# One channel tile of the convolution on GpSimd, and narrower chunk pair products, in the two mixers

## The chip, the cores and the metric

The kernel runs on one core of a Trainium2 chip. The metric is the device time of one execution in microseconds (us), of the slowest core, which here is the only one; of several runs the median counts. The engines of the core are TensorE (PE in the profile, its weight loads PEld), VectorE (DVE), ScalarE (ACT), GpSimd (POOL) and SyncE (SP, which here only issues transfers).

## What is computed

Two transformer layers with four parallel mixers each (the first followed by a dense feed-forward network, the second by a mixture of experts), and then one more block of another kind. The change is in the mixers alone, which run twice:

```python
for l in range(DEPTH):                       # DEPTH = 2, x: 256 tokens x 1024 channels
    h = _rmsnorm(x, norm_mix[l])
    p_rw, p_sb, p_ret, p_conv = jnp.split(h @ w_in[l], MIX_SPLITS, axis=-1)
    branches = (_rwkv7_mixer(p_rw, ...), _stick_breaking_mixer(p_sb, ...),
                _retention_mixer(p_ret, ...), _conformer_conv_mixer(p_conv, ...))
    merged = sum over i of jax.nn.sigmoid(h @ w_gate[l, i]) * (branches[i] @ w_branch[l, i])
    x = x + merged @ w_out[l]
    ...

def _conformer_conv_mixer(p, dw, db, ln_w, ln_b):
    u_a, u_b = jnp.split(p, 2, axis=-1)
    u = u_a * jax.nn.sigmoid(u_b)
    u = lax.conv_general_dilated(u, dw[:, None, :], ..., padding=[(CONV_WIDTH - 1, 0)],
                                 feature_group_count=BRANCH_WIDTH) + db
    return jax.nn.silu(_layernorm(u, ln_w, ln_b, CONV_LN_EPS))

def _rwkv7_mixer(p, ...):                     # 4 heads of 64 channels
    def step(state, inp):                     # one step per token
        r_t, w_t, k_t, v_t, kk_t, a_t = inp
        sa = jnp.einsum('bhvk,bhk->bhv', state, -kk_t)
        state = (state * w_t[:, :, None, :] + sa[..., None] * (kk_t * a_t)[:, :, None, :]
                 + v_t[..., None] * k_t[:, :, None, :])
        return state, jnp.einsum('bhvk,bhk->bhv', state, r_t)
```

The convolution is depthwise: every one of 256 channels has 31 weights of its own (CONV_WIDTH) and sums 31 shifted copies of its row of 256 tokens. The recurrence of the first mixer is computed by the kernel in 8 chunks of 32 tokens, from products of all pairs of tokens of a chunk.

## The kernel before

Activations lie with channels on the partitions, so the 256 channels of a branch are two tiles (index `j`) of 128 partitions by 256 tokens. Weights come from HBM as blocks of 128x1024 in a ring. A block is used in split form: ScalarE copies its rounded part (`HiParts.upto`, L343), VectorE subtracts that from the block (`LoParts.upto`, L363), and TensorE makes three products of each (`three_passes`, L270 to L272). `upto(n)` on either engine means: split all blocks up to number n that are not yet split. Each engine has its own program, written out by hand in the order in which it runs; waits are on counters of named steps (`after(name)`), and on VectorE every instruction of the mixers waits for the one before it (`link`).

The stage at issue stands in `mix_section`. TensorE runs, for each chunk c of 8, `gram(c)` and `gate(c)`. `gate(c)` projects one block of gate weights: 24 products of 128x256. `gram(c)` makes the pair products of the chunk. Its operands `KR` and `BK` hold the four heads on a block diagonal: for tile j (heads 2j and 2j+1) a 128x128 matrix whose only filled columns are the 64 of these two heads (32 tokens for each head); the rest is zero. There are four products of 128x256 into bank Z0 or Z1 (L632, 2 of w by 2 of j, the two j added up in PSUM), two of 128x128 into bank X (L639, again added over j), and four transposes (L646).

VectorE runs beside it, for each chunk c: the masked product of the bank (`gram_c`, L1067, from bank Z and constants), for c = 3 and 7 another one from bank X (`A_0`, `A_1`), the split of the block for the next gate, and four of the 31 taps of the convolution by `taps`, each for both tiles: `acc[j] = u[j] shifted by k, times weight, plus acc[j]`, one instruction on 128x256 (L1071; the first tap L1069). The input of the convolution, `u`, is finished by the instruction just ahead of this stage. The result `acc` is read first by the two instructions of `conv_y` (L1069 too), much later: behind the four steps of the inverse of chunks 0 to 3 (`inverse(0, k)`, `squares(0, k)`, `ret_s`).

After the chunks TensorE runs `ret_scores(0)` (L687, L688), then `squares(0, 1)` (L666 into bank C, L671 into bank X), `gate(8)`, and `inverse(0, 1)` (L680). L671 needs bank X, which VectorE has read when `A_1` is done. A scratch tile `at_`, which lies over `u`, is used for the weights of two of the four retention heads.

GpSimd does little: it writes zeros over `praw`, `KR`, `BK` and the margin of `u` at the start of a mixer section (L474 to L478), and scales eight tiles for the router (L1448).

Of the kernel before, what the change touches and what calls it, by code (L numbers as in the profile page):

```python
# [15 lines left out]
ALU = mybir.AluOpType  # L16
# [4 lines left out]
T = 256  # L21
# [6 lines left out]
HD = 64  # L28
# [6 lines left out]
TAPS = 31  # L35
PAD = TAPS - 1
# [94 lines left out]


SPARE_AT = 28704
PARAMS2_AT = 29120


class Plan:
# [9 lines left out]
    def done(self, engine, name=None, by=1):  # L147
        self.count[engine] += by
        if name:
            assert (self.section, name) not in self.steps, name  # L150
            self.steps[self.section, name] = (engine, self.count[engine])
        return self.sem[engine], by

    def after(self, name, section=None):
        engine, n = self.known[section or self.section, name] if self.known is not None else ("pe", 1)
        return self.sem[engine], n
# [250 lines left out]
def mix_section(env, layer):  # L407

    nc, dram, x, banks, h_hi, h_lo = (env[n] for n in ("nc", "dram", "x", "banks", "h_hi", "h_lo"))
    after, done, C, eps, ident, col, plan = (env[n] for n in ("after", "done", "C", "eps", "ident", "col", "plan"))  # L410
    first = MIX1_AT if layer else 0
    P0, P1, Z0, Z1, BO, BC, BY, BX = (banks[n] for n in ("P0", "P1", "Z0", "Z1", "O", "C", "Y", "X"))
    pair = lambda b: b.rearrange("p (j t) -> p j t", j=2)
    quad = lambda b: b.rearrange("p (j t) -> p j t", j=4)

    cut = carver(env)
    prm = env["params"][:, layer]
    R = lambda name, i=0, n=1: col(prm, PCOL, name, i, n)
# [3 lines left out]
    KR = cut(2, NCH, 2, P)  # L422
    BK = cut(2, 2, NCH, P)
# [19 lines left out]
    sbv, rv = values[:, 0], values[:, 1]  # L443
    rg, acc, scr = (cut(2, T) for _ in range(3))
    u = cut(2, PAD + T)
    az = cut(384)
    dec = cut(2, NCH)
    w0h, small = cut(4), cut(64)
    assert cut.at[0] <= SPARE_AT, cut.at[0]

    uflat, rflat = u.rearrange("p j t -> p (j t)"), rv.rearrange("p a t -> p (a t)")
    A1 = sbo.rearrange("p j t -> p (j t)").rearrange("p (i n) -> p i n", i=4)
    exz = vv.rearrange("p j t -> p (j t)")[:, 0:384]
    at_ = uflat[:, 0:384]
# [16 lines left out]
    def gpsimd(g):  # L471
        if layer:
            g.wait_ge(*after("h2_lo_3", "mix0"))
        g.memset(praw[:, :, 0:1], 0.0).then_inc(*done("pool", "praw_zeroed"))  # L474
        if layer == 0:
            g.memset(KR, 0.0).then_inc(*done("pool"))
        g.memset(BK, 0.0).then_inc(*done("pool"))
        g.memset(u[:, :, 0:PAD], 0.0).then_inc(*done("pool", "zeroed"))  # L478

    def tensor(pe):  # L480
        blocks = Blocks(env, pe, first)
# [31 lines left out]
        for k in range(KD):  # L513
# [4 lines left out]
            mm = pe.matmul(BX[:, 0:T], C("ones"), sqx[:, k, :], start=(k == 0), stop=(k == KD - 1))  # L518
# [28 lines left out]
        for j in range(2):  # L547
            mm = pe.matmul(Z0[:, j * T:(j + 1) * T], lora[0:64, j * P:(j + 1) * P], pm[0:64, 4, :], start=True, stop=True)
        mm.then_inc(*done("pe", "lora_w"))
        take(Z1, "tha")  # L550
        for j in range(2):
            mm = pe.matmul(Z1[:, j * T:(j + 1) * T], lora[64:128, j * P:(j + 1) * P], pm[64:128, 4, :], start=True,
                           stop=True)
# [9 lines left out]
        for j in range(2):  # L563
            mm = pe.matmul(BO[:, j * T:(j + 1) * T], lora[:, 256 + j * P:256 + (j + 1) * P], pm[:, 5, :], start=True, stop=True)
# [11 lines left out]
        for a in range(TT2):  # L576
            for j in range(2):
                mm = pe.transpose(BY[:, (2 * a + j) * P:(2 * a + j + 1) * P], vv[:, j, a * P:(a + 1) * P], ident)
# [48 lines left out]
        def gram(c):  # L627
            z = Z0 if c % 2 == 0 else Z1
            take(z, f"gram_{c}")
            for w in range(2):  # L630
                for j in range(2):
                    mm = pe.matmul(z[:, w * T:(w + 1) * T], BK[:, w, j, c, :],  # L632
                                   KR[:, j, c].rearrange("p w n -> p (w n)"), start=(j == 0), stop=(j == 1))
            mm.then_inc(*done("pe", f"p_gram_{c}"))

            if c % 4 == 0:
                take(BX, f"A_{c // 4}")
            for j in range(2):
                mm = pe.matmul(quad(BX)[:, c % 4, :], KR[:, j, c, 0, :], BK[:, 0, j, c, :], start=(j == 0), stop=(j == 1))  # L639
            if c % 4 == 3:  # L640
                mm.then_inc(*done("pe", f"p_A_{c // 4}"))
            o = BO if c % 2 == 0 else BC
            take(o, f"BK_{c}")
            for w in range(2):
                for j in range(2):
                    mm = pe.transpose(quad(o)[:, 2 * w + j, :], BK[:, w, j, c, :], ident)  # L646
            mm.then_inc(*done("pe", f"p_BK_{c}"))
# [43 lines left out]
        def attend(hh, values, weights, ready, out_name):  # L691

            b, j = (hh % 2) * HD, hh // 2
            pe.wait_ge(*after(ready))
            pe.matmul(BO[b:b + HD, j * T:(j + 1) * T], values[:, 0, hh * HD:(hh + 1) * HD], weights[:, 0:T],
                      start=True, stop=False, skip_group_check=True)
            pe.matmul(BO[b:b + HD, j * T + P:(j + 1) * T], values[:, 1, hh * HD:(hh + 1) * HD], weights[:, T:T + P],
                      start=False, stop=True, skip_group_check=True).then_inc(*done("pe", out_name))
# [7 lines left out]
        for k in range(1, 5):  # L706
            inverse(0, k)
            if k < 4:
                squares(0, k + 1)
            attend(k - 1, rv, az if k % 2 else at_, f"ret_s_{k - 1}", f"p_ret_o_{k - 1}")  # L710
            if k < 4:
                ret_scores(k)
            gate(8 + k)
# [17 lines left out]
        for j in range(2):  # L731
            mm = pe.matmul(Z0[:, 0:T], C("ones"), acc[:, j, :], start=(j == 0), stop=(j == 1))
# [5 lines left out]
        for j in range(2):  # L738
            mm = pe.matmul(Z1[:, 0:T], C("ones"), scr[:, j, :], start=(j == 0), stop=(j == 1))
# [321 lines left out]
    def vector(v):  # L1061
# [112 lines left out]
            tt(out, out, scr, ADD, name + "_in")  # L1174
        lo.upto(28)
        v.wait_ge(*after("conv_b"))
        stt(u[:, :, PAD:PAD + T], acc, 1.0, u[:, :, PAD:PAD + T], ADD, MUL)

        def taps(first, last):
            for k in range(first, last):  # L1180
                for j in range(2):
                    w = R("dw", j * TAPS + k)
                    if k == 0:
                        ts(acc[:, j, :], u[:, j, 0:T], w, None, MUL)
                    else:
                        stt(acc[:, j, :], u[:, j, k:k + T], w, acc[:, j, :], MUL, ADD)

        for c in range(NCH):
            lo.upto(28 + c)
# [21 lines left out]
            tt(t, t, quad(BY), ADD, f"TI_{g}_{k}")  # L1211

        def ret_s(hh):
            z, out = (Z0, Z1)[hh % 2], (az, at_)[hh % 2]
            v.wait_ge(*after(f"p_ret_s_{hh}"))
            if hh >= 2:
                v.wait_ge(*after(f"p_ret_o_{hh - 2}"))
            d = C("decay", hh * T, T)
            tt(out[:, 0:T], z[:, 0:T], d, MUL)
            tt(out[:, T:T + P], z[:, T:T + P], d[:, 0:P], MUL, f"ret_s_{hh}")  # L1220
# [25 lines left out]
        for k in range(1, 5):  # L1246
            inverse_add(0, k)
            lo.upto(37 + k)
            if k < 3:
                mt_copy(0, k + 1)  # L1250
            if k < 4:
                ret_s(k)
        for j in range(2):
            ts(acc[:, j, :], acc[:, j, :], 0.5, R("conv_b", j), MUL, ADD, name="conv_y" if j else None)
        mt_copy(1, 1)
# [1496 lines left out]
```

## Time and profile before

| | |
|---|---|
| median of 3 runs | 1684.46 us (1684.11 to 1688.5) |
| profiled execution | 1684.62 us |
| its span, first to last instruction | 1682.8 us |
| TensorE products busy | 1564.1 us, 93% |
| TensorE weight loads busy | 1355.7 us, 81% |
| VectorE busy | 1131.3 us, 67% |
| ScalarE busy | 822.2 us, 49% |
| GpSimd busy | 18.3 us, 1% |

Products overlap, so a busy TensorE is not one at its peak; the distance between the starts of two products tells how fast it goes. TensorE has two clock levels, 2.4 and 1.2 GHz; the profile gives the granted clock as a share of the higher one. The 1.82 us between span and time lie outside the program.

The convolution stage of the first layer lies at 122 to 172 us of the span, that of the second at 679 to 729 us.

### The profile page before, as it was taken

The page shows a single profiled execution, that of the slowest core. Times are in us where ns is not written, and L with a number is a line of the kernel's source. Part 1 is how long each engine was busy: PE and PEld are TensorE (multiplying, and loading weights), DVE is VectorE, ACT ScalarE, POOL GpSimd, SP SyncE. Part 2 cuts the span into 40 slices and gives each one's busy share as a digit, 9 for nine tenths or more (in the row PEclk, how much of TensorE's full clock was granted, in tenths as well). Part 3 has the DMA queues.
Part 4 walks back from the last instruction along what each step waited for, and adds up shares of the span by engine and source line. Part 5 has one row for each costly group of instructions (what it writes and reads, how often), then busy time and mean ns, then how long its engine had stood idle before and what let it go on. Part 6 is the DMA issues. An engine that isn't in the chain of part 4 may idle for free. (4 is left out here: it accounts for less than half of the span.)

```text
span 1682.8 us, 24848 instructions
## 1 busy us (share of the span) xinstructions
PE 1564.1 (93%) x10030; PEld 1355.7 (81%) x10030; DVE 1131.3 (67%) x1633; ACT 822.2 (49%) x1084; POOL 18.3 (1%) x21
## 2 busy tenths in 40 slices
PE   7889989989999899988999699999999989988998
PEld 6778979879999888987988477777777769976677
DVE  6689564665555668966455698888888876267535
ACT  4643334434444464323542677777776754354322
POOL 1000000000000000000000100000000000000000
PEclk9999999999999999999999799999999999879899
DMA  7432222345555344222325099999999974412122
GB/s 280 149 114 88 82 94 88 115 137 167 185 188 195 126 139 150 88 76 75 114 88 201 20 339 340 339 338 345 363 340 344 336 253 163 151 63 76 63 77 74
DMA packets 82052, 292.96 MB, mean 174 GB/s; under 512 B 9095, under 2 KB 11647, under 8 KB 81679
## 3 DMA queue, kind: packets, MB, share of 16 engines
q1 hardware_dynamic: 81935, 291.34, 49.2%
q8 instruction: 81, 1.33, 0.3%
q14 instruction: 36, 0.29, 0.1%
HBM read 290.22 MB, written 1.08 MB: 173 GB/s over the span
## 5 line engine op out<-in xcount | busy, mean ns | idle before, releaser
L363 DVE TENSOR_TENSOR ring_lo<-ring,weights_hi 128x1024 fp32r<-128x1024 f32 x359 | 433.4, 1222 | 269.3 <-ACT weights_hi L343 266.5
L270 PE MATMUL bank_P<-h_hi,weights_hi 128*128 128x256 f32 x1584 | 472.9, 299 | 37.7 <-DVE h_lo L1067 18.9
L343 ACT ACTIVATE weights_hi<-ring 128x1024 fp32r<-128x1024 f32 x359 | 372.3, 1056 | 225.0 <-PE bank_P L272 187.4
L272 PE MATMUL bank_P<-h_hi,ring_lo 128*128 128x256 f32 x1584 | 456.3, 288 | 0.0
L271 PE MATMUL bank_P<-h_lo,weights_hi 128*128 128x256 f32 x1584 | 455.4, 288 | 0.0
L270 PEld LDWEIGHTS bank_P<-h_hi,weights_hi 128*128 128x128 f32 x1584 | 309.7, 196 | 54.4 <-issue 26.9
L272 PEld LDWEIGHTS bank_P<-h_hi,ring_lo 128*128 128x128 f32 x1584 | 313.6, 198 | 0.0
L271 PEld LDWEIGHTS bank_P<-h_lo,weights_hi 128*128 128x128 f32 x1584 | 310.2, 196 | 1.7 <-issue 1.0
L271 PE MATMUL bank_P<-ring_lo,gathered_hi 128*96 128x512 f32 (+1 forms) x384 | 144.0, 375 | 0.0
L363 DVE TENSOR_TENSOR ring_lo<-ring,tokens_hi 128x1024 fp32r<-128x1024 f32 x76 | 90.4, 1217 | 2.3 <-ACT tokens_hi L343 2.3
L363 DVE TENSOR_TENSOR ring_lo<-ring,tokens_lo 128x1024 fp32r<-128x1024 f32 x74 | 88.2, 1217 | 2.3 <-ACT tokens_lo L343 2.3
L271 PEld LDWEIGHTS bank_P<-ring_lo,gathered_hi 128*96 128x96 f32 x384 | 62.2, 162 | 20.8
L1071 DVE SCALAR_TENSOR_TENSOR arena<-arena,mixer_params 128x256 f32<-128x256 f32 (+1 forms) x152 | 74.7, 491 | 4.9
L343 ACT ACTIVATE tokens_hi<-ring 128x1024 fp32r<-128x1024 f32 x76 | 77.2, 1049 | 0.0
L343 ACT ACTIVATE tokens_lo<-ring 128x1024 fp32r<-128x1024 f32 x74 | 75.2, 1049 | 0.0
L620 PE MATMUL bank_P<-arena,ring 128*128 128x256 f32 x256 | 63.4, 409 | 5.7 <-DVE arena L1071 5.7
L620 PEld LDWEIGHTS bank_P<-arena,ring 128*128 128x128 f32 x256 | 52.3, 208 | 15.3 <-DVE arena L1071 7.3
L270 PE MATMUL bank_P<-weights_hi,gathered_hi 128*96 128x512 f32 (+1 forms) x158 | 60.7, 384 | 1.7 <-DVE gathered_lo L1734 1.7
L884 ACT ACTIVATE arena<-bank_P 128x512 f32<-128x512 f32 x58 | 34.6, 596 | 53.2 <-PE bank_P L272 52.7
L884 ACT ACT_TABLE_LOAD x41 | 52.6, 1283 | 15.1 <-DVE arena L1069 7.5
L272 PE MATMUL bank_P<-weights_hi,gathered_lo 128*96 128x512 f32 (+1 forms) x158 | 59.7, 378 | 0.0
L1067 DVE TENSOR_TENSOR arena<-arena 128x512 f32<-128x512 f32 (+1 forms) x90 | 53.6, 595 | 8.4 <-ACT arena L884 5.8
(485 smaller groups left out, 2598.9 us busy)
## 6 DMA issues: line engine op xcount, KB each, us to landing
ring<-stream SPq DMA_DIRECT2D x541, 512.0 KB, 4.4
cst<-consts SPq DMA_DIRECT2D x1, 1712.0 KB, 10.3
arena<-params SPq DMA_DIRECT2D x1, 1211.0 KB, 7.2
arena<-x SPq DMA_DIRECT2D x1, 1024.0 KB, 5.0
arena<-bias_vec SPq DMA_DIRECT2D x8, 128.0 KB, 3.1
out<-arena SPq DMA_DIRECT2D x2, 512.0 KB, 2.6
arena<-params SPq DMA_DIRECT2D x2, 256.0 KB, 7.4
arena<-bias_vec SPq DMA_DIRECT2D x8, 64.0 KB, 2.8
```

The costliest lines, as they stand in the source:

```text
L270: pe.matmul(out, hi, x_hi, start=start, stop=False, skip_group_check=True)
L271: pe.matmul(out, hi, x_lo, start=False, stop=False, skip_group_check=True)
L272: return pe.matmul(out, lo, x_hi, start=False, stop=stop, skip_group_check=True)
L343: a.activation(self.slots[i % len(self.slots)], env["ring"][:, slot, :], ACT.Copy)\
L363: v.tensor_tensor(env["ring_lo"][:, slot, :], env["ring"][:, slot, :], self.slots[i % len(self.slots)].bitcast(F32), ALU.subtract).then_in ...
L620: mm = pe.matmul(bank[:, j * T:(j + 1) * T], w[c][:, d * P:(d + 1) * P], y[:, c, :], start=(c == 0), stop=(c == 1))
L884: link(a.activation(out, in_, func, **kw), name)
L1067: tt = lambda out, a0, a1, op, name=None: link(v.tensor_tensor(out, a0, a1, op), name)
L1071: v.scalar_tensor_tensor(out=out, in0=a0, scalar=s, in1=a1, op0=op0, op1=op1), name)
```

## The change

It has three parts, the same in both layers.

GpSimd computes tile 1 of the convolution, for all 31 taps, in two instructions for each tap: a product with the weight into a scratch tile `scaled` (two buffers, in free space), and an addition to `acc[:, 1]`. VectorE keeps tile 0. `conv_y` waits for the last tap. GpSimd waits for a completed product ahead of each addition, and for the addition two taps back ahead of each product.

The pair products take only the 64 filled columns of a tile: L632 becomes four products of 128 columns (2 of 64), L639 two of 64, and none adds to another.

The retention weights of heads 1 and 3 go to `exz` in place of `at_`, since `u` is now still being read by GpSimd.

```diff
+SCALED_AT = 29728
...
+    cut.at[0] = SCALED_AT
+    scaled = cut(2, T)
...
         g.memset(u[:, :, 0:PAD], 0.0).then_inc(*done("pool", "zeroed"))
+        g.wait_ge(*after("conv_in"))
+        for k in range(TAPS):
+            w = R("dw", TAPS + k)
+            if k == 0:
+                g.tensor_scalar(acc[:, 1, :], u[:, 1, 0:T], w, None, ALU.mult).then_inc(*done("pool", "tap_0"))
+            else:
+                if k > 2:
+                    g.wait_ge(*after(f"tap_{k - 2}"))
+                g.tensor_scalar(scaled[:, k % 2, :], u[:, 1, k:k + T], w, None, ALU.mult).then_inc(*done("pool", f"scaled_{k}"))
+                g.wait_ge(*after(f"scaled_{k}"))
+                g.tensor_tensor(acc[:, 1, :], acc[:, 1, :], scaled[:, k % 2, :], ALU.add).then_inc(*done("pool", f"tap_{k}"))
...
             for w in range(2):
                 for j in range(2):
-                    mm = pe.matmul(z[:, w * T:(w + 1) * T], BK[:, w, j, c, :],
-                                   KR[:, j, c].rearrange("p w n -> p (w n)"), start=(j == 0), stop=(j == 1))
+                    own = slice(j * HD, (j + 1) * HD)
+                    mm = pe.matmul(quad(z)[:, 2 * w:2 * w + 2, own], BK[:, w, j, c, :], KR[:, j, c, :, own], start=True, stop=True)
...
             for j in range(2):
-                mm = pe.matmul(quad(BX)[:, c % 4, :], KR[:, j, c, 0, :], BK[:, 0, j, c, :], start=(j == 0), stop=(j == 1))
+                own = slice(j * HD, (j + 1) * HD)
+                mm = pe.matmul(quad(BX)[:, c % 4, own], KR[:, j, c, 0, :], BK[:, 0, j, c, own], start=True, stop=True)
...
-            attend(k - 1, rv, az if k % 2 else at_, f"ret_s_{k - 1}", f"p_ret_o_{k - 1}")
+            attend(k - 1, rv, az if k % 2 else exz, f"ret_s_{k - 1}", f"p_ret_o_{k - 1}")
...
-        stt(u[:, :, PAD:PAD + T], acc, 1.0, u[:, :, PAD:PAD + T], ADD, MUL)
+        stt(u[:, :, PAD:PAD + T], acc, 1.0, u[:, :, PAD:PAD + T], ADD, MUL, "conv_in")
 
         def taps(first, last):
             for k in range(first, last):
-                for j in range(2):
-                    w = R("dw", j * TAPS + k)
-                    if k == 0:
-                        ts(acc[:, j, :], u[:, j, 0:T], w, None, MUL)
-                    else:
-                        stt(acc[:, j, :], u[:, j, k:k + T], w, acc[:, j, :], MUL, ADD)
+                w = R("dw", k)
+                if k == 0:
+                    ts(acc[:, 0, :], u[:, 0, 0:T], w, None, MUL)
+                else:
+                    stt(acc[:, 0, :], u[:, 0, k:k + T], w, acc[:, 0, :], MUL, ADD)
...
-            z, out = (Z0, Z1)[hh % 2], (az, at_)[hh % 2]
+            z, out = (Z0, Z1)[hh % 2], (az, exz)[hh % 2]
...
+        v.wait_ge(*after(f"tap_{TAPS - 1}"))
         for j in range(2):
             ts(acc[:, j, :], acc[:, j, :], 0.5, R("conv_b", j), MUL, ADD, name="conv_y" if j else None)
```

VectorE's program in the chunks of the first layer, in instructions of the same form in a row (names are output and inputs; `arena` is the large scratch memory in which `acc`, `u` and most tiles lie, `cst` the constants, `mixer_params` the weights of the taps). Before:

```order
L363 TENSOR_TENSOR ring_lo<-ring,weights_hi 128x1024
L1071 SCALAR_TENSOR_TENSOR arena<-arena,mixer_params 128x256 x8
L1067 TENSOR_TENSOR arena<-bank_Z,cst 128x512
L1067 TENSOR_TENSOR arena<-bank_X,cst 128x512
L363 TENSOR_TENSOR ring_lo<-ring,weights_hi 128x1024
```

The same place after the change (where the lines have other numbers):

```order
L364 TENSOR_TENSOR ring_lo<-ring,weights_hi 128x1024
L1086 SCALAR_TENSOR_TENSOR arena<-arena,mixer_params 128x256 x4
L1082 TENSOR_TENSOR arena<-bank_Z,cst 128x512
L1082 TENSOR_TENSOR arena<-bank_X,cst 128x512
L364 TENSOR_TENSOR ring_lo<-ring,weights_hi 128x1024
```

Four of eight taps of a chunk are gone from VectorE; nothing else moved on it. GpSimd's program from the first layer's zeros on, before:

```order
L478 MEMSET arena 128x2x30
L474 MEMSET arena 128x8
L477 MEMSET arena 128x4096
L478 MEMSET arena 128x2x30
```

And after, with its first taps:

```order
L481 MEMSET arena 128x2x30
L486 ISA
L486 TENSOR_SCALAR arena<-arena,mixer_params 128x256
L490 TENSOR_SCALAR arena<-arena,mixer_params 128x256
L492 TENSOR_TENSOR arena<-arena 128x256
L490 TENSOR_SCALAR arena<-arena,mixer_params 128x256
L492 TENSOR_TENSOR arena<-arena 128x256
```

Behind the zeros now stand 61 instructions for each layer, 31 products and 30 additions. TensorE's pair products of one chunk, before:

```order
L632 MATMUL bank_Z<-arena 128x256 x4
L639 MATMUL bank_X<-arena 128x128 x2
L646 MATMUL bank_O<-cst,arena 128x128 x4
```

And after:

```order
L647 MATMUL bank_Z<-arena 128x2x64 x4
L654 MATMUL bank_X<-arena 128x64 x2
```

Only the widths change there; each product appears in the trace as two instructions.

## Rows read from the trace of the kernel before

**Rows 1.** The page: the span, and busy time, share and instructions of each engine.
```profile
span 1682.8 us, 24848 instructions
PE 1564.1 (93%) x10030; PEld 1355.7 (81%) x10030; DVE 1131.3 (67%) x1633; ACT 822.2 (49%) x1084; POOL 18.3 (1%) x21
```
**Rows 2.** Stretches (us): each engine's busy time and count, granted clock, transfers.
```profile
core 0: us, PE busy (x) PEld busy (x) DVE busy (x) ACT busy (x) POOL busy (x), PEclk, DMA share, GB/s
124.00:146.00 22.00, 22.00 (x164) 21.05 (x163) 20.86 (x37) 7.84 (x10) 0.00 (x0) 1.00 0.30 99
170.00:172.00 2.00, 2.00 (x11) 2.00 (x11) 1.89 (x4) 1.06 (x1) 0.00 (x0) 0.50 0.55 195
```
**Rows 3.** Timeline of DVE: start and length in us, then the instructions, merged.
```profile
122.36 0.68 DVE L1071 SCALAR_TENSOR_TENSOR arena<-arena 128x512 f32<-128x512 f32 x1
123.08 0.69 DVE L1067 TENSOR_TENSOR arena<-bank_Z,cst 128x512 f32<-128x512 f32 x1
...
135.59 1.23 DVE L363 TENSOR_TENSOR ring_lo<-ring,weights_hi 128x1024 fp32r<-128x1024 f32 x1
136.73 4.12 DVE L1071 SCALAR_TENSOR_TENSOR arena<-arena,mixer_params 128x256 f32<-128x256 f32 x8
140.89 0.69 DVE L1067 TENSOR_TENSOR arena<-bank_Z,cst 128x512 f32<-128x512 f32 x1
...
166.45 0.69 DVE L1067 TENSOR_TENSOR arena<-bank_X,cst 128x512 f32<-128x512 f32 x1
```
**Rows 4.** Timeline of PE, pair products, then L671 and products behind it.
```profile
135.26 1.89 PE L632 MATMUL bank_Z<-arena 128*128 128x256 f32 x8
136.99 0.61 PE L639 MATMUL bank_X<-arena 128*128 128x128 f32 x4
137.43 0.60 PE L646 MATMUL bank_C<-cst,arena 128*128 128x128 f32 x4
...
140.71 1.89 PE L632 MATMUL bank_Z<-arena 128*128 128x256 f32 x8
...
167.19 2.08 PE L671 MATMUL bank_X<-arena 128*128 128x128 f32 x8 [2.57 <-DVE arena L1067]
168.92 0.56 PE L270 MATMUL bank_P<-h_hi,weights_hi 128*128 128x256 f32 x1
...
173.61 0.61 PE L680 MATMUL bank_Y<-arena 128*128 128x128 f32 x4
...
723.81 1.16 PE L671 MATMUL bank_X<-arena 128*128 128x128 f32 x8 [2.58 <-DVE arena L1067]
724.73 0.36 PE L270 MATMUL bank_P<-h_hi,weights_hi 128*128 128x256 f32 x1
```
**Rows 5.** Timeline of PE, products of 128 and of 64 columns.
```profile
180.99 1.05 PE L680 MATMUL bank_Y<-arena 128*128 128x128 f32 x8
181.88 1.13 PE L666 MATMUL bank_C<-arena 128*128 128x128 f32 x8
...
248.56 0.39 PE L784 MATMUL bank_C<-arena 128*128 128x64 f32 x2
248.79 0.39 PE L785 MATMUL bank_C<-arena 128*128 128x64 f32 x2
```
**Rows 6.** Timeline of POOL.
```profile
379.55 3.52 POOL L477 MEMSET arena<- 128x4096 f32 x1
...
923.76 7.22 POOL L1448 TENSOR_SCALAR arena<-x_chan,mixer_params 128x256 f32<-128x256 f32 x8 [540.61 <-DVE x_chan L1071]
```
**Rows 7.** Timeline of DVE beside these instructions of POOL, and just behind.
```profile
379.85 2.36 DVE L363 TENSOR_TENSOR ring_lo<-ring,weights_hi 128x1024 fp32r<-128x1024 f32 x2 [0.40 <-ACT weights_hi L343]
...
929.64 0.38 DVE L1538 MAX8 arena<-arena 128x8 f32<-128x8 f32 x2
...
930.60 0.41 DVE L1541 CAST arena<-arena 128x2 f32<-128x2 uint32 x1
...
932.61 0.17 DVE L1541 CAST arena<-arena 128x2 f32<-128x2 uint32 x1
```
**Rows 8.** Timeline of DVE at `conv_y` of the first layer.
```profile
199.77 0.73 DVE L1069 TENSOR_SCALAR arena<-arena,mixer_params 128x256 f32<-128x256 f32 x2
```

## Prediction

> **What bounds the kernel now.** The page comes first: TensorE is busy 93% of the span, VectorE 67%, GpSimd 1% [rows 1]. That does not yet say what a change in the mixers is worth, so the stretches of the convolution stage are next. At 124 to 146 us TensorE has no idle time at full clock, but VectorE is busy 20.86 of 22 us [rows 2]: two engines side by side, nearly equally loaded. The timelines tell which is slower. TensorE starts the pair products of a chunk at 135.26 and of the next at 140.71, a period of 5.45 us [rows 4]. VectorE runs the same chunk from 135.59 (block split) over eight taps to the masked product, which ends at 141.6: 1.14 + 4.16 + 0.73 = 6.03 us [rows 3]. So VectorE falls back 0.58 us with each chunk, unseen as long as the banks and split blocks are a chunk ahead; at the end TensorE pays: L671 waits 2.57 us for the product that VectorE ends at 167.14 (and 2.58 us in the second layer) [rows 3, 4]. In the first layer the clock falls as well, to 0.50 at 170 to 172 [rows 2], the lower level, after that idle time: L671's eight instructions take 1.73 us up to the next start there and 0.92 in the second layer [rows 4].
>
> So both halves of the change aim at the right place: VectorE is the bound of this stage, TensorE is next by 0.58 us for each chunk.
>
> **Pair products.** Eight instructions of 256 columns take 1.73 us (135.26 to 136.99) [rows 4]. Eight of 128 columns take 0.89 us (180.99 to 181.88) [rows 5]. That is 0.84 us less for each chunk. L639 takes 0.44 us for four of 128 columns, 0.11 each [rows 4]; two of 64 columns take 0.23, 0.11 each too [rows 5], so halving their columns gives nothing. In `gram(0)` the saving ends in a wait that is already there. For seven chunks it is 5.9 us for each layer, and TensorE's period becomes 4.61 us. It counts only if VectorE keeps up.
>
> **Taps taken from VectorE.** Eight taps take 4.12 us, 0.515 each [rows 3]. Four less is 2.06 us of 6.03: alone, VectorE would need 3.97 us for a chunk, less than TensorE's 4.61. Then TensorE would be the bound, and both the wait for L671 (2.57 us a layer) and the fallen clock would go: 0.8 us at L671, and 1.8 us in `gate(8)`, which takes 4.69 us there (168.92 to 173.61) and some 2.9 in a chunk (137.8 to 140.71) [rows 4].
>
> **Taps added to GpSimd.** Its only product on such a tile takes 7.22/8 = 0.90 us [rows 6]. No row shows an addition on it. The bounds: writing a tile alone, 3.52 us for 4096 columns [rows 6] or 0.22 us for 256; and two inputs each at the price of the one-input product, 1.8 us. I take 0.90, the row with the same tile. With 0.1 us allowed for the wait on its own product, 30 pairs and the first product take 0.9 + 30 x 1.9 = 58 us. It can start at 123.04 [rows 3] and is due at 199.77, `conv_y` [rows 8]: 76.7 us, or some 65 if the stage ahead gets 11 us shorter. The wait at `conv_y` thus costs nothing by itself. If it did, the splits for gates 13 and on are queued behind it on VectorE, and with them TensorE. The zeros that it writes first are done long before 122 us.
>
> **What GpSimd does to VectorE.** This is the term that decides. One row shows both at work with something in SBUF to share: the CAST of L1541 starts at 930.60 and takes 0.41 us; the same instruction takes 0.17 us two microseconds later [rows 7]. It ends at 931.01, just when GpSimd's eight products end (923.76 + 7.22 = 930.98) [rows 6]. It reads as if VectorE was held until GpSimd's instruction was over. Other pairs show no effect: MAX8 takes 0.19 us beside the same products, and two block splits beside the zeros take 1.18 us each, as ever [rows 7]; the zeros read nothing. A tap or block split, with two inputs in SBUF, beside a GpSimd instruction that reads SBUF has no row. Its cost is between nothing and the whole remaining GpSimd instruction. I take the whole, as in the CAST's row.
>
> The Trainium skill, "SBUF — State Buffer", section "Who interferes with whom", says that a VectorE instruction with two SBUF inputs contends with a GpSimd instruction that reads SBUF, that it does not with one that only writes, and that the second one to issue is blocked until the first is finished. The CAST's row and the splits beside the zeros agree with it; by this rule the change loses time, without it it gains.
>
> Worked out: VectorE and GpSimd then take turns, since at the end of one's instruction the other's is already waiting. A chunk on VectorE has five instructions with two SBUF inputs (split, four taps) and one with an input in PSUM (masked product, 0.73 us), beside which GpSimd may run. Each of the five waits for one GpSimd instruction of 0.90, one of which runs beside the masked product: 3.97 + 5 x 0.90 - 0.73 = 7.74 us, against 6.03. From 123.08 to `A_1` there are seven such chunks: 7 x 1.71 = 12 us later. GpSimd has then done about 37 of its 61 instructions. The last three taps, the split and the first two masks of the inverse wait for it six times more, 5.4 us; some 3.5 us of that is hidden by `squares(0, 1)` and `gate(8)` on TensorE, 2 remain. The last 18 run beside an inverse in which VectorE has idle time, and end near 200, ahead of `conv_y`, now due near 213. TensorE is idle nearly 3 us in each chunk, so its own 0.84 us saved give nothing. Sum: 14 us for each layer, 28 in all, on 1684.6 us of the profiled execution (the median is 0.2 us lower): **1713 us**. The idle time could bring the lower clock into this stage; nothing in the rows says that it must (second layer: same wait, no fall), so it is in the range only, at up to 5 us a layer.
>
> The Trainium skill, "GPSIMD Engine Reference", section 3.1, has 4497 ns for a GpSimd `tensor_tensor` of 2048 columns. Scaled to 256 columns that is an estimate of 0.56 to 0.65 us for the addition. The period would still be near 7.6 us, since a second, shorter instruction then fits in ahead of the split, and the sum about 1709. No run here shows it so far.
>
> The retention weights in `exz` cost nothing: same shape, and no one reads that tile there.
>
> **Rivals.**
> 1. *No contention for these instructions* (chance 0.22). The splits and MAX8 at unchanged length speak for it, one CAST against. Each layer wins 5.9 + 2.6 us, the first 2.6 more of clock: 11.1 + 8.5 = 19.6, so 1665 us.
> 2. *Short holds* (0.16). GpSimd holds VectorE only for a part of its instruction, say half, 0.45 us. Nothing says when in its 0.90 us the hold begins; the CAST began in the second half of one. Period 3.97 + 4 x 0.45 = 5.8 us (the fifth hides behind the masked product): 1.6 us a layer less than before, perhaps 1 in the inverse and the clock back; 1680 us, with 1665 and 1695 at its ends.
> 3. *GpSimd is late* (0.10). VectorE's next instruction always wins, or the addition costs 1.8 us without contention. GpSimd then ends 14 to 20 us after a `conv_y` that has moved up to 188.7: with 45 instructions left at 160 us it ends near 203; with 30 pairs of 2.8 us near 208. TensorE waits behind it. Net of the 11 us won, 4 to 8 us a layer: 1692 to 1700 us. It decides once GpSimd needs over 65 us for its work.
>
> **Numbers.** The forecast, full holds, has 0.50, with 1700 to 1735 about it (additions of 0.4 to 1.2 us, clock); additions of 1.8 us with full holds, 10 us a chunk, would be over 1740 and have 0.02 in it. Slower: 0.50 + 0.10 + 0.04 of rival 2 + 0.02 left over = 0.66. Within 0.3% (5 us, about what a measurement of this kernel can tell from no change): 0.07. Faster: 0.22 + 0.05 of rival 2 = 0.27. Slower cases alone do not make up 8 in 10, so the range takes in rival 1: 1663 to 1735.
>
> **What the profile after would show.** Taps on VectorE of 1.2 to 1.5 us in place of 0.48 and splits of about 2 in place of 1.2 in the stage, periods of 7.7 us, TensorE waiting for splits (L270 for L363's new line) for 2 to 3 us in each chunk, L671 some 12 us later. If taps stay at 0.48 and periods are 4.6, rival 1 is right; taps near 0.9, rival 2; a wait for GpSimd at `conv_y`, rival 3. The pair products should take 0.89 us in any case. Outside the mixers nothing should change; a difference there would make the sum wrong.

## The result, and the profile after the change

The changed kernel takes **1673.99 us** (median of 7 runs, 1672.05 to 1678.14) against 1684.11 us of the kernel before (median of 7, 1681.71 to 1688.5). The ratio is 0.9938, with a 95% interval of 0.9922 to 0.9954. It is 10 us faster, where 28 us slower was forecast. A second measurement of it, on the chip of a later group of experiments, gave 0.9948 (0.9931 to 0.9964).

The page of the profiled execution, with the totals that answer to [rows 1], and the group of GpSimd's products:

```profile
span 1673.8 us, 24908 instructions
PE 1553.6 (93%) x10030; PEld 1347.7 (81%) x10030; DVE 1118.5 (67%) x1571; ACT 822.1 (49%) x1084; POOL 146.3 (9%) x143
...
L490 POOL TENSOR_SCALAR arena<-arena,mixer_params 128x256 f32<-128x256 f32 x60 | 73.9, 1232 | 0.0
```

VectorE lost 62 taps, 32 us of work by the 0.515 us of [rows 3], but its busy time fell by 12.8 us only. The rest came back as longer instructions. One chunk on VectorE's timeline, against 6.03 us in [rows 3]:

```profile
145.24 1.22 DVE L364 TENSOR_TENSOR ring_lo<-ring,weights_hi 128x1024 fp32r<-128x1024 f32 x1
146.38 2.98 DVE L1086 SCALAR_TENSOR_TENSOR arena<-arena,mixer_params 128x256 f32<-128x256 f32 x4
149.39 0.69 DVE L1082 TENSOR_TENSOR arena<-bank_Z,cst 128x512 f32<-128x512 f32 x1
150.12 1.22 DVE L364 TENSOR_TENSOR ring_lo<-ring,weights_hi 128x1024 fp32r<-128x1024 f32 x1
```

From split to split it is 4.88 us. The four taps take 2.98 us, where 2.06 would be undisturbed. Looked at one by one they are not alike:

```profile
146.38 0.96 DVE L1086 SCALAR_TENSOR_TENSOR arena<-arena,mixer_params 128x256 f32<-128x256 f32 x1
147.38 0.58 DVE L1086 SCALAR_TENSOR_TENSOR arena<-arena,mixer_params 128x256 f32<-128x256 f32 x1
147.99 0.49 DVE L1086 SCALAR_TENSOR_TENSOR arena<-arena,mixer_params 128x256 f32<-128x256 f32 x1
148.52 0.84 DVE L1086 SCALAR_TENSOR_TENSOR arena<-arena,mixer_params 128x256 f32<-128x256 f32 x1
```

GpSimd's timeline beside them (L490 a product, L492 an addition):

```profile
144.17 1.09 POOL L490 TENSOR_SCALAR arena<-arena,mixer_params 128x256 f32<-128x256 f32 x1
145.35 1.71 POOL L492 TENSOR_TENSOR arena<-arena 128x256 f32<-128x256 f32 x1
147.04 1.09 POOL L490 TENSOR_SCALAR arena<-arena,mixer_params 128x256 f32<-128x256 f32 x1
148.22 0.86 POOL L492 TENSOR_TENSOR arena<-arena 128x256 f32<-128x256 f32 x1
```

The two long taps (0.96 and 0.84) lie beside additions. The tap of 0.58 runs wholly inside a product (147.04 to 148.13), and is only 0.09 us longer than usual. The tap of 0.49, the usual length, starts at the end of that product and ahead of the next addition. The addition of 1.71 us lies beside a block split: there GpSimd was the one held. So the two engines do hold each other up, but only a part of the time.

TensorE's timeline in the first layer:

```profile
117.24 1.05 PE L647 MATMUL bank_Z<-arena 128*128 128x128 f32 x8
...
121.65 0.36 PE L271 MATMUL bank_P<-h_hi,weights_hi 128*128 128x256 f32 x1 [2.52 <-DVE ring_lo L364]
...
126.00 1.15 PE L647 MATMUL bank_Z<-arena 128*128 128x128 f32 x8
...
130.65 1.05 PE L647 MATMUL bank_Z<-arena 128*128 128x128 f32 x8
...
135.22 1.05 PE L647 MATMUL bank_Z<-arena 128*128 128x128 f32 x8
...
160.60 1.16 PE L686 MATMUL bank_X<-arena 128*128 128x128 f32 x8 [0.45 <-DVE arena L1082]
...
164.97 1.13 PE L695 MATMUL bank_Y<-arena 128*128 128x128 f32 x8 [0.37 <-DVE arena L1082]
167.58 1.13 PE L681 MATMUL bank_C<-arena 128*128 128x128 f32 x8 [1.49 <-issue]
```

The chunk is 4.57 us now (5.45 in [rows 4]) and TensorE waits for nothing from the end of `gate(0)` to the end of the eight chunks. L686, in the place of L671, waits 0.45 us and not 2.57. But `gate(0)` at 121.65 waited 2.52 us for its block split (1.64 before), and it lasts until 126.00, 4.35 us, where other gates take 2.92: the clock has fallen in it. The table of stretches (columns as in [rows 2]) has 0.60 there and full clock later:

```profile
122.00:126.00 4.00, 4.00 (x25) 4.00 (x24) 3.90 (x6) 1.06 (x1) 2.66 (x2) 0.60 0.38 131
130.00:144.00 14.00, 14.00 (x125) 14.00 (x124) 13.51 (x18) 6.19 (x8) 13.50 (x13) 1.00 0.39 129
```

GpSimd's last addition and VectorE's `conv_y`, which waits for it, stand 4 us apart, so that wait costs nothing:

```profile
188.71 1.13 POOL L492 TENSOR_TENSOR arena<-arena 128x256 f32<-128x256 f32 x1
```
```profile
193.86 0.73 DVE L1084 TENSOR_SCALAR arena<-arena,mixer_params 128x256 f32<-128x256 f32 x2
```

### The profile page after: what moved, and what is told of

Read it like the earlier page. It is cut to its first block and busy times, and to the rows that moved or that the text cites. A ratio compares the mean times of both kernels' runs of the same rounds, so it can differ in the third digit from the quotient of the medians.

```text
span 1673.8 us, 24908 instructions
## 1 busy us (share of the span) xinstructions
PE 1553.6 (93%) x10030; PEld 1347.7 (81%) x10030; DVE 1118.5 (67%) x1571; ACT 822.1 (49%) x1084; POOL 146.3 (9%) x143
## 5 line engine op out<-in xcount | busy, mean ns | idle before, releaser
L490 POOL TENSOR_SCALAR arena<-arena,mixer_params 128x256 f32<-128x256 f32 x60 | 73.9, 1232 | 0.0
L1086 DVE SCALAR_TENSOR_TENSOR arena<-arena,mixer_params 128x256 f32<-128x256 f32 (+1 forms) x92 | 57.8, 628 | 2.8
```

Source lines behind the costliest of these rows:

```text
L490: g.tensor_scalar(scaled[:, k % 2, :], u[:, 1, k:k + T], w, None, ALU.mult).then_inc(*done("pool", f"scaled_{k}"))
L1086: v.scalar_tensor_tensor(out=out, in0=a0, scalar=s, in1=a1, op0=op0, op1=op1), name)
```

## Experiments

Whole times of one kernel scatter by 3 to 11 us from run to run, so beside the measured times one **stretch** is used: from the start of the rotation's product (115.32 us before) to the start of the convolution's sum (217.03 us before), 101.7 us in each layer of the kernel before. It holds the convolution stage and the inverse, and it repeats to 0.1 us (95.59 and 95.64 in two profiles of the changed kernel). The table has all kernels, the one before first and the others roughly in the order of their stretch. Each ratio is to runs of the kernel before in the same group of experiments (their medians lie between 1684.05 and 1685.27 us). Where a row has two kernels, the stretches are those of the first; the second's differ from them by at most 0.05 us.

| kernel | stretch, layer 1 / 2 (us) | median (us) | ratio to before | 95% interval |
|---|---|---|---|---|
| before | 101.71 / 101.72 | 1684.11 | 1 | |
| e1 narrow pair products only | 101.79 / 101.78 | 1684.13 | 1.0002 | 0.9993 to 1.0011 |
| e9 before, with an early split | 99.61 / 99.61 | 1679.31 | 0.9969 | 0.9958 to 0.9981 |
| e2, e7 divided convolution only | 96.22 / 96.22 | 1670.86, 1674.2 | 0.9924, 0.9934 | 0.9908 to 0.994, 0.9921 to 0.9946 |
| changed; e6 the same again | 95.59 / 95.61 | 1673.99, 1676.29 | 0.9938, 0.9948 | 0.9922 to 0.9954, 0.9931 to 0.9964 |
| e8 divided convolution, early split | 95.20 / 94.34 | 1667.15 | 0.9892 | 0.9878 to 0.9907 |
| e10 changed, products for additions | 91.81 / 91.80 | 1665.32 | 0.9889 | 0.987 to 0.9907 |
| e4, e12 changed, early split | 91.61 / 92.44 | 1664.73, 1666.08 | 0.989, 0.9884 | 0.9874 to 0.9906, 0.9869 to 0.9898 |
| e3 changed, no GpSimd taps | 91.59 / 91.59 | 1663.28 | 0.988 | 0.9865 to 0.9896 |
| e11 changed, early split, late mask | 89.77 / 89.76 | 1661.16 | 0.9861 | 0.9844 to 0.9878 |

### Each half alone

**e1**, the narrower pair products in the kernel before:

```diff
-                    mm = pe.matmul(z[:, w * T:(w + 1) * T], BK[:, w, j, c, :],
-                                   KR[:, j, c].rearrange("p w n -> p (w n)"), start=(j == 0), stop=(j == 1))
+                    own = slice(j * HD, (j + 1) * HD)
+                    mm = pe.matmul(quad(z)[:, 2 * w:2 * w + 2, own], BK[:, w, j, c, :], KR[:, j, c, :, own], start=True, stop=True)
```

> Only the narrower pair products; both channel tiles of the convolution stay on VectorE. Theory A (VectorE bounds the stage, and each half of the change frees only its own engine): VectorE's chunk stays at 6.03 us, so TensorE's saved 0.84 us a chunk end in a longer wait at L671's place: 2.57 + 5.9 = 8 us or so. Time within 2 us of before (1682 to 1686). Theory B (the gain came mostly from the narrower products): 5.9 us a layer, 12 in all, 1672.

1.0002. TensorE's timeline at L671's place (here L672):

```profile
167.51 2.08 PE L672 MATMUL bank_X<-arena 128*128 128x128 f32 x8 [4.68 <-DVE arena L1068]
```

It starts at 167.51 against 167.19 [rows 4], after a longer wait. Smaller waits ahead of it (1.77 and 0.56 us), the longer wait of `gate(0)` (2.52 us for 1.64) and its fallen clock took the rest of the saving. VectorE bounds the stage, and theory A holds for this half.

**e2**, the changed kernel with the wide pair products put back (the diff above, reversed).

> Only the convolution is divided; pair products stay 256 columns wide. Theory A: TensorE's chunk of 5.45 us becomes the bound; the wait of 2.6 us a layer before L671 and the fallen clock behind it (2.6 us, first layer) go, VectorE's delays by GpSimd stay hidden: 1684 - 5.2 - 2.6, some 1676 to 1679. Theory B: 1684 or slower. The wait of gate(0) for its block split stays 1.6 us at full clock, as before.

The stretch of 96.2 is 5.5 us shorter than before; by it, 11 us. The median moved by 13.5. Without the narrower products `gate(0)` waits 1.64 us and stays at full clock:

```profile
118.70 0.36 PE L271 MATMUL bank_P<-h_hi,weights_hi 128*128 128x256 f32 x1 [1.64 <-DVE ring_lo L364]
121.62 1.89 PE L646 MATMUL bank_Z<-arena 128*128 128x256 f32 x8
```

So nearly the whole gain is the divided convolution's. The size was more than expected, and it was not plain whether this kernel even beats the changed one. **e6** and **e7** are the two again, on one chip.

> The changed kernel itself, on the same chip as the next three. From its stretch between the rotation's product and the convolution's sum (95.6 us against 101.7, twice) the time should be 12 us under before: 1672 to 1675.

> Only the convolution divided, again, beside the changed kernel. Theory E (the narrower products are worth the 0.6 us a layer that the stretch shows, 96.2 against 95.6; the 3 us by which this kernel was faster before lay outside it and are noise of chip and run): 1 us slower than the changed kernel. Theory F (the narrower products make the kernel slower by 3 us, through the fallen clock in gate(0)): 3 us faster than the changed kernel.

Their intervals overlap. The kernel with wide products had the lower median both times, by 3.1 us in two different groups and by 2.1 us side by side, though its stretch is 0.6 us longer in each layer. The difference lies between the layers' stretches, in code that is the same in both: 455.1 and 455.0 us there in the changed kernel's two profiles, 450.0 and 453.4 in the other's. Over all kernels of the study that distance scatters from 450.0 to 457.6 us in no order that the change would explain (454.9 in the kernel before). So it stays open whether one of the two is faster. By the stretches the narrower products bring 1.2 us in both layers together, and the whole times do not show even that.

### What contention costs

**e3**, the changed kernel without GpSimd's taps (it leaves tile 1 of the convolution out):

```diff
-        g.wait_ge(*after("conv_in"))
-        for k in range(TAPS):
...
-        v.wait_ge(*after(f"tap_{TAPS - 1}"))
```

> As the changed kernel, but the 61 GpSimd instructions of each layer are left out: tile 1 is not convolved, and nothing waits for it. What is left is the changed kernel without any contention. Theory C (contention still costs part of the gain, through the masks and block splits at the head of the inverse): taps at 0.48 us, the waits of 0.45, 0.37 and 1.49 us there gone and another microsecond behind: 2 to 3.5 us a layer faster than the changed kernel, 1667 to 1670. Theory D (contention is hidden, the missing gain is the wait and fallen clock of gate(0)): same as the changed kernel, 1674.

The stretch is 4.0 us shorter than the changed kernel's, 8 us in all, and the median 1663.28: theory C, somewhat above its size. VectorE's four taps take 2.05 us again:

```profile
144.98 2.05 DVE L1075 SCALAR_TENSOR_TENSOR arena<-arena,mixer_params 128x256 f32<-128x256 f32 x4
```

`gate(0)` still waits 2.52 us in it. So contention costs 4.0 us of each layer's stretch, and it is not the whole difference to the best kernel below.

Where it costs them is seen from TensorE's starts, counted from the rotation's product. At the first squares behind the chunks (L681) the two kernels are level, 43.46 us with GpSimd's taps and 43.47 without. At L686 the changed kernel is 0.6 us later, at the second squares 3.0 us (52.05 against 49.09), at the end 4.0 us. In the eight chunks themselves contention cost TensorE nothing: VectorE's 4.88 us are only 0.31 us more than TensorE's 4.57, and it had a lead.

**e5**, a probe of the hold itself, run ahead of all other work in the changed kernel: VectorE does short additions of 64 columns, one after the other, while GpSimd works.

```diff
+        for i in range(32):
+            link(v.tensor_tensor(dv[2][:, 0:64], dv[0][:, 0:64], dv[1][:, 0:64], ALU.add))
...
+        for i in range(6):
+            last(g.tensor_scalar(pl[2][:, 0:256], pl[0][:, 0:256], w, None, ALU.mult), i, 6, 4)
```

> The changed kernel with a probe ahead of all other work: VectorE runs short additions of 64 columns with two inputs in SBUF, one by one, beside GpSimd's products and additions of 256 and 1024 columns, and beside its zeros; then one-input instructions beside GpSimd additions. (Its time is longer by the probe.) Theory H1 (GpSimd holds the shared way into SBUF only while its columns stream: some 0.2 us of a product's 0.92 and 0.4 of an addition's 0.73 at 256 columns): most short additions take their usual 0.2 us, one for each GpSimd instruction is longer, by up to 0.2 us beside products and 0.4 beside additions, four times that at 1024 columns; none beside zeros. Theory H2 (the hold is the whole instruction): one short addition for each GpSimd instruction takes 0.8 to 1.0 us, at 256 columns, and no more than one starts during any of GpSimd's instructions. One-input instructions outside PSUM of the scalar kind: delayed in the same way; reciprocals: not.

Groups by line of VectorE, with durations in ns (least, median, most). In this order: alone; beside products of 1024 columns; additions of 1024; products of 256; additions of 256; zeros of 1024; then products by a scalar of 64 columns beside additions of 1024, and reciprocals beside the same:

```profile
L460 DVE TENSOR_TENSOR arena<-arena x12: 224/226/226, 4.4 to 7.2; 128x64 f32<-128x64 f32 x12
...
L466 DVE TENSOR_TENSOR arena<-arena x24: 224/226/1080, 25.8 to 33.5; 128x64 f32<-128x64 f32 x24
...
L470 DVE TENSOR_TENSOR arena<-arena x24: 224/226/2383, 33.9 to 44.0; 128x64 f32<-128x64 f32 x24
...
L474 DVE TENSOR_TENSOR arena<-arena x32: 224/226/466, 44.4 to 53.9; 128x64 f32<-128x64 f32 x32
...
L478 DVE TENSOR_TENSOR arena<-arena x32: 224/226/767, 54.3 to 65.5; 128x64 f32<-128x64 f32 x32
...
L482 DVE TENSOR_TENSOR arena<-arena x16: 224/226/226, 65.9 to 69.8; 128x64 f32<-128x64 f32 x16
...
L486 DVE TENSOR_SCALAR arena<-arena x24: 254/254/2377, 70.1 to 80.9; 128x64 f32<-128x64 f32 x24
...
L490 DVE RECIPROCAL arena<-arena x24: 553/553/553, 81.3 to 94.8; 128x64 f32<-128x64 f32 x24
```

The hold is the longest less 0.226. GpSimd's own lengths come from its timeline: products 0.92 us for 256 columns and 2.84 for 1024, additions 0.72 and 2.34.

| GpSimd instruction | its length | hold | share |
|---|---|---|---|
| product, 256 columns | 0.92 | 0.24 | 26% |
| product, 1024 columns | 2.84 | 0.85 | 30% |
| addition, 256 columns | 0.72 | 0.54 | 75% |
| addition, 1024 columns | 2.34 | 2.16 | 92% |
| zeros, 1024 columns | 0.95 | 0 | |

A product holds VectorE near its start and then no more. The held addition starts at 45.67, so its 0.24 us are over at 45.91; the product runs on until 46.50, and the next short addition runs free beside it:

```profile
45.58 0.92 POOL L436 TENSOR_SCALAR arena<-arena 128x256 f32<-128x256 f32 x1
```
```profile
45.67 0.46 DVE L474 TENSOR_TENSOR arena<-arena 128x64 f32<-128x64 f32 x1
46.17 0.23 DVE L474 TENSOR_TENSOR arena<-arena 128x64 f32<-128x64 f32 x1
```

An addition holds it nearly to its end, by the same reckoning until 55.22 + 0.54 = 55.76 of 55.90, and no short addition runs free inside it:

```profile
55.18 0.72 POOL L439 TENSOR_TENSOR arena<-arena 128x256 f32<-128x256 f32 x1
```
```profile
55.22 0.77 DVE L478 TENSOR_TENSOR arena<-arena 128x64 f32<-128x64 f32 x1
```

H1 is right for products, in size too. For additions the truth lies between the two: 0.54 us, where H1 had 0.4 and H2 the whole 0.72. VectorE's products by a scalar are held as well (2.38 us for 0.25), its reciprocals never.

**e10** tests this in place: the same number of GpSimd instructions, all of them products (tile 1 is then no convolution).

```diff
-                g.tensor_tensor(acc[:, 1, :], acc[:, 1, :], scaled[:, k % 2, :], ALU.add).then_inc(*done("pool", f"tap_{k}"))
+                g.tensor_scalar(acc[:, 1, :], scaled[:, k % 2, :], w, None, ALU.mult).then_inc(*done("pool", f"tap_{k}"))
```

> The changed kernel in which GpSimd's 30 additions a layer are products too (tile 1 of the convolution is then not the reference's; the number and order of GpSimd's instructions stay). If a product holds VectorE for 0.24 us and an addition for its whole 0.5 to 0.7 us, as the probe shows, VectorE's chunk goes from 4.87 us to some 4.4, below TensorE's 4.57, and the masks at the head of the inverse lose less: stretch 95.6 - 2 to 4 = 92 to 93.5 us, time 1666 to 1670. If every GpSimd instruction costs VectorE alike, by its length (products are the longer ones): stretch 96 or more, 1674 or slower.

The stretch falls to 91.8 us, within 0.2 us of the kernel without any GpSimd taps, and the time to 1665.32. Four taps take 2.28 us, and VectorE waits for blocks:

```profile
147.27 1.23 DVE L364 TENSOR_TENSOR ring_lo<-ring,weights_hi 128x1024 fp32r<-128x1024 f32 x1 [0.21 <-ACT weights_hi L344]
148.41 2.28 DVE L1086 SCALAR_TENSOR_TENSOR arena<-arena,mixer_params 128x256 f32<-128x256 f32 x4
```

GpSimd is busy for longer in this kernel (155.3 us for 146.3), yet its cost is nearly gone. So the cost came from GpSimd's additions and not from how long GpSimd works; this is shown. That it is their second input that does it, and not something else in which an addition differs from a product by a scalar, is likely but not shown: no other two-input instruction was run on GpSimd.

### The wait of gate(0)

**e4** moves one call on VectorE, into the idle time that [rows 3] leave ahead of the rotation's product:

```diff
             tt(out, raw, cos, MUL)
+            lo.upto(28)
             v.wait_ge(*after(swap))
```

> The changed kernel with the split of the blocks of gate(0) and gate(1) moved on VectorE into its idle 2.6 us ahead of the rotation's product, some 6 us earlier. Theory D: gate(0) no longer waits 2.5 us, the clock no longer falls in it (1.4 us), and VectorE reaches the stage 2.3 us earlier: 2.3 to 3.9 us a layer, 1666 to 1669. If the wait only moves to the next split or bank: 1672 to 1675.

Both splits now end before 116.3 us, beside a wait that VectorE had anyway, and TensorE goes from the pair products straight into the gate:

```profile
113.93 2.36 DVE L364 TENSOR_TENSOR ring_lo<-ring,weights_hi 128x1024 fp32r<-128x1024 f32 x2
```
```profile
118.38 0.61 PE L661 MATMUL bank_O<-cst,arena 128*128 128x128 f32 x4
118.74 0.36 PE L271 MATMUL bank_P<-h_hi,weights_hi 128*128 128x256 f32 x1
```

The stretch falls by 4.0 and 3.2 us, and the time to 1664.73 us. In the second layer it falls by less because the clock falls behind a wait of 1.49 us at the head of the inverse (L681's eight instructions take 1.53 us to the next start there and 0.97 in the first layer, behind the same wait):

```profile
708.49 1.74 PE L681 MATMUL bank_C<-arena 128*128 128x128 f32 x8 [1.49 <-issue]
710.02 1.92 PE L686 MATMUL bank_X<-arena 128*128 128x128 f32 x8
```

Theory D holds too. C and D were no rivals: taking away the contention alone is worth 4.0 us a layer, and moving the split alone 3.2 to 4.0. No run has both, so it is not shown that the two add up. **e8** and **e9** make the same move without the narrower products, and in the kernel before.

> Wide products, convolution divided, and the split for gate(0) moved ahead of the rotation's product. Stretch: 96.2 less the wait of 1.6 us, with VectorE (4.9 us a chunk) still ahead of TensorE (5.45): 94 to 95 us, so 1669 to 1671. The kernel with narrower products and early split has 91.6 there: if this one has 94.5, the narrower products are worth 3 us a layer once gate(0) does not wait, against 0.6 with the wait.

> The kernel before with that split moved and nothing else. VectorE reaches the stage 2.4 us earlier and, as the bound of it, leaves it 2.4 us earlier: stretch 101.7 - 2.4 = 99.3, or 97 if the clock does not fall behind L671 any more; 1675 to 1680. If VectorE were not the bound: unchanged, 1684.

e8 gains 1.0 and 1.9 us of stretch by it, e9 2.1. With the early split the narrower products are worth 3.6 us in the first layer and 1.9 in the second (95.20 and 94.34 against 91.61 and 92.44), without it 0.6, and in the kernel before nothing. The split has to be early for them to count, since otherwise their first saving only lengthens the wait of `gate(0)`, and the clock falls behind that longer wait.

### A version that beats both

What is left of contention shows at the head of the inverse, where TensorE waited 0.37 and 1.49 us in e4 as in the changed kernel, and not at all in e3. **e11** moves VectorE's mask for chunks 4 to 7 out of the way, on top of e4; **e12** is e4 again, beside it.

```diff
         inverse_start(0)
-        inverse_start(1)
         ret_s(0)
         mt_copy(0, 1)
         lo.upto(37)
+        inverse_start(1)
```

> As the changed kernel with the early split, and VectorE's second mask at the head of the inverse (for chunks 4 to 7, needed some 40 us later) moved behind the first copy and block split. If the waits of 0.4 and 1.5 us that TensorE has at the first step of the inverse come from VectorE being late there (two masks of 1.06 us each instead of 0.7, beside GpSimd): 1 to 1.5 us a layer less in the stretch, 90.5 against 91.6 to 92.4; 2 to 3 us faster than the next kernel. If they come from elsewhere: the same as it.

> The changed kernel with the early split again, on the same chip as the one ahead: stretch 91.6 to 92.4 in both layers, 1664 to 1667.

The wait of 1.49 us is down to 0.22:

```profile
160.40 1.13 PE L695 MATMUL bank_Y<-arena 128*128 128x128 f32 x8 [0.37 <-DVE arena L1082]
161.75 1.13 PE L681 MATMUL bank_C<-arena 128*128 128x128 f32 x8 [0.22 <-issue]
```

1661.16 us, 0.9861 of before (0.9844 to 0.9878), against 1666.08 for e12. Every run of e11 was faster than every run of e12. The gain is more than was expected: 1.8 us of stretch in the first layer and 2.7 in the second, where the clock now stays up as well. It is the fastest kernel of the study, 23 us under before.

## Why the prediction was wrong

The forecast had the sign wrong, 28 us slower where it got 10 us faster. That the measured time lies inside the range of 1663 to 1735 is no merit of its sum; the range had been stretched to take in rival 1.

**What bounds the stage** was right: e1 alone shows that VectorE did, with a saving of TensorE that left the time unchanged (1.0002), and e9 agrees, where VectorE's earlier start gave 2.1 us a layer.

**The step that failed is "Each of the five waits for one GpSimd instruction of 0.90".** VectorE's chunk was forecast at 7.74 us and takes 4.88. Two sizes in it were wrong. First, the hold: I took the whole instruction, from one row, a CAST beside a product. A product of 256 columns holds a two-input instruction for 0.24 of 0.92 us, near its start. Second, the addition: it takes 0.72 us, not 0.90, and holds for 0.54. The estimate of 0.56 to 0.65 us, from the Trainium skill, "GPSIMD Engine Reference", section 3.1, was nearer than my nearest row. The turns were wrong also: in the chunk shown, two taps wait for an addition (0.48 and 0.36 us more than usual), one meets a product and loses 0.09, one loses nothing, and the split waits for nothing, but holds GpSimd's addition (1.71 us). Measured, contention adds 0.92 us to the taps of a chunk, not 3.8. VectorE then falls behind TensorE by 0.31 us a chunk, and the 12 us that were to be lost in the chunks were not lost at all.

The CAST does not fit the probe either. Its delay, 0.41 - 0.17 = 0.24 us, has the size of a product's hold, but not its place: it started some 0.54 us into the last product and was held to that product's end [rows 6, 7], where the probe's additions ran free. It did the same in the changed kernel. So it is held in another way than a two-input addition, and was no row for a tap. Why it is held so late stays open.

The rule of the Trainium skill, "SBUF — State Buffer", section "Who interferes with whom", is borne out in kind by e5: two inputs in SBUF contend with GpSimd's reading, zeros and reciprocals do not, products by a scalar do. But its exclusive lock, by which the second engine is blocked "until the first finishes" (the same page of the Trainium skill, section "Summary: rules for kernel authors"), holds nearly for GpSimd's additions and not for its products, where the second engine goes on after a quarter of the instruction. The measurement decides.

**Rival 2** (short holds, 1680 us, 1665 to 1695) described the mechanism, though its period of 5.8 us was too long as well; it had a chance of 0.16 for want of any row on when a hold begins. **Rival 3** did not occur: GpSimd ended 4 us ahead of `conv_y`.

**Rival 1** without contention gave 1665; e3, which is that kernel, measured 1663.28. The terms for what is saved were right in sum, 19.6 us forecast and 20.2 by the stretches, but that is in part luck. The forecast was 11.1 us for the first layer, 2.6 of them for the fallen clock, and 8.5 for the second; e3 saves 10.1 in each. In the kernel before the clock falls behind L671 in the first layer alone, and yet both stretches are 101.7 us, since in the second TensorE waits at the head of the inverse instead:

```profile
729.00 1.13 PE L680 MATMUL bank_Y<-arena 128*128 128x128 f32 x8 [1.20 <-DVE arena L1067]
731.08 1.13 PE L666 MATMUL bank_C<-arena 128*128 128x128 f32 x8 [0.95 <-issue]
```

At L666 both layers are level again (59.18 and 59.15 us behind the rotation's product). The fallen clock was hidden behind VectorE there, and to win it back was worth nothing by itself. These 2.15 us of waiting stood nowhere in the sum for the second layer; nor did what the next paragraph tells of `gate(0)`, which took about as much away.

**The narrower products** do take 0.89 us for 1.73, as forecast. L639's take 0.39 us for 0.44 (136.11 to 136.50 in the changed kernel), where nothing less was forecast, so TensorE's chunk is 4.57 us and not 4.61. But "in `gram(0)` the saving ends in a wait that is already there" was only half of it: the wait grew from 1.64 to 2.52 us and the clock fell behind it, which cost 1.43 us in `gate(0)` of the first layer and 1.5 in that of the second. The sum had no term for it.

**The inverse's head** was named ("the first two masks of the inverse wait for it"), with 2 us left for TensorE. By e3 it is 3.0 us at the second squares, 0.37 + 1.49 of them in two waits. This is the one place of the forecast loss that was real; e11 gives back 1.8 to 2.7 us of it in the stretch.

The ledger for the first layer, TensorE's starts relative to the rotation's product (115.32 before, 115.53 after): at the second pair products +1.4 us; at the last −3.8; at L671's place −6.8; at the second squares −7.1; at the convolution's sum −6.1. Twice that is 12.2 us, of which the profiled execution kept 9.0 and the medians 10.1. Some 2.7 us of the difference lie in the last block, which the change doesn't touch (311.5 us before, 314.2 after, and 311.5 to 314.5 in the others without order).

## What to carry to other kernels

Work moved to GpSimd costs VectorE by which instructions GpSimd runs, and not by how long it runs: here a product by a scalar was nearly free beside VectorE, a two-input addition was not. When a step is shortened just ahead of a wait, look whether the longer idle time brings the clock down; moving the awaited step into idle time elsewhere was worth more than the shortening. A delay on one engine is no loss until it outruns the lead that the engine has; here eight chunks with contention cost TensorE nothing. And a bound taken from one row should say which instruction that row has seen, and when in the other's run: mine was a CAST late in a product, and I priced five two-input instructions by it.

## What the runs showed of the hardware

- GpSimd's product with a scalar from SBUF holds VectorE's two-input instructions for 0.24 us at 256 columns and 0.85 at 1024, near its start; its addition for 0.54 and 2.16 us, nearly to its end (e5). It takes 0.92 and 2.84, and 0.72 and 2.34 us: the two-input one is the shorter at the same width.
- The same addition took 1.71 us beside VectorE's block split: the hold works both ways.
- A CAST of VectorE that started some 0.54 us into a product of 256 columns on GpSimd took 0.41 us in place of 0.17 and ended with the product [rows 6, 7]; two-input additions that started there took their usual 0.226 us (e5).
- TensorE's clock fell to the lower level in `gate(0)` after a wait of 2.52 us (0.60 on average from 122 to 126 us), in both layers of all five profiles with narrow products and a late split (changed, e1, e3, e6, e10). It did not after the wait of 1.64 us at the same place, in both layers of the kernel before, e2 and e7. But it fell after a wait of 2.57 us in the first layer of the kernel before, and not after one of 2.58 us in the second [rows 4]; and after one of 1.49 us in the second layer of e4, and not in the first. The length of the wait alone does not decide it.
- Products of 64 columns take little less than those of 128 (L639: 0.39 us for four against 0.44); narrowing them brought 0.05 us a chunk.
